# First quarter of w_ada by row blocks on an encoder layer kernel, and ScalarE's statistics of x moved ahead

## The chip, the cores and the metric

The kernel runs on one core of one Trainium2 chip. The metric is the device time of one execution in microseconds (us); less is better. Each time in the text is of one core; nothing is shared with other cores.

## The reference, cut to what matters

One encoder layer with 512 tokens of width 1024, batch 1, all f32. What the change touches is the beginning:

```python
mod = jnp.einsum('bd,de->be', jax.nn.silu(c), w_ada[l]) + b_ada[l]      # c: (1, 1024), w_ada: (1024, 6144)
sh_a, sc_a, g_a, sh_f, sc_f, g_f = jnp.split(mod[:, None, :], 6, axis=-1)
h = _layer_norm(x) * (1.0 + sc_a) + sh_a                                # needs the first third of mod
proj = h @ w_in[l]                                                      # 512 x 1024 by 1024 x 3072
```

Behind it come eight heads of neighbourhood attention, four heads of differential attention, an output projection with a layer norm, and PEER: for each token and each of eight heads 16 experts are chosen, and their rows of two tables of 16384 x 1024 are gathered, multiplied and added up. The output is one (1, 512, 1024) array.

## The kernel before, in words

The five engines have a program each, written out by hand, and wait for one another by semaphores. TensorE goes through a list of groups (`FIRST_GROUPS`, lines 118 to 138): two small transposes (columns of c and b_ada, and the neighbourhood bias), four `na_table` groups of eight products of a 32 x 128 by a 32 x 60 block (L721), the eight transposed blocks of the normalised x (`h_act` and `h_dve`, L744), then the stream of projections of w_in and "ada" groups, then attention. Each group has one of six banks of PSUM in turn, and it may start when the group that had the bank before has been evacuated by ScalarE or VectorE (`wait_for_bank`, L645). From the gather phase on, the expert rows come by indirect DMA issued by GpSimd (L623), VectorE makes the dot products (L1379) and TensorE the weighted sums (L837).

**Weights.** w_ada is 1024 x 6144, cut into twelve chunks of 512 columns (2 MB each), and w_in into six. They go through five slots of SBUF in the order of `STREAM` (L59 to 61): w_ada's chunks 0 to 3, then a chunk of w_in, two of w_ada, and so on. SP issues the loads (`load_chunk`, L467). A chunk is laid out as eight blocks of 128 rows side by side, so each partition gets eight runs of 512 f32 (2 KB). Chunks 0 to 3 are the first 2048 columns: sh_a and sc_a. Their slots are free for the next loads when the semaphore `mod_summed` is up (L461).

**The first 2048 columns of mod.** VectorE sums each chunk over its eight row blocks, each times its column of silu(c) (`sum_chunk`, L1202): one `tensor_scalar` (L1210) and seven `scalar_tensor_tensor` (L1212) of 128 x 512, each linked to the one before by a semaphore. The sums still have to be added up over the 128 partitions, and shift and scale are wanted as columns: that is `mod_columns` (L636), four products a chunk of a 128 x 128 block of the sum with a column of ones, each of which writes one column of `mod_ps` (L640). An f32 product stands as two instructions in the profile. It comes in TensorE's program behind the group ("h_dve", 6), and when chunk 3 is through, `mod_summed` rises. VectorE adds b_ada (L1230, L1231), `mod_ready` rises, and ScalarE and VectorE evacuate the transposed blocks of x with the scale and the shift in them (L968, L1252). The first projection (L754) takes them as they come, and needs the first chunk of w_in.

**Statistics of x.** ScalarE's own queue carries, before anything else, the loads of `na_place`, of the four 128-row tiles of x (L866), of `t5_place`, `t5_bias` and the sub-keys. Tiles 0 and 1 have their mean and variance from VectorE (L1068, L1221; the semaphore is `x_agg`). Tiles 2 and 3 have them from ScalarE: in front of the evacuation of `na_table` 2, ScalarE sums the tiles (L954), waits for the mean from GpSimd (L565), sums the squares of the differences (L958), and then normalises all four tiles (L962) as GpSimd delivers shift and inverse deviation (L566 to L575). TensorE's transposes of x wait for the four normalised tiles (L741).

**Order on VectorE:** statistics of tiles 0 and 1, sums of chunks 0 to 3 (a small copy behind chunk 1), the addition of b_ada, the evacuations. **Order on SP:** small loads, five chunks, the lambda rows, and, once `na_table` 3 is through, `mods` (b_ada's other rows), then the further chunks as slots come free.

## Time and profile before

| | us |
|---|---|
| median of 3 runs | 1751.28 |
| lowest and highest of them | 1751.17, 1754.83 |
| profiled execution, span from its first to its last instruction | 1756.3 |
| TensorE busy | 1479.7 (84%) |
| VectorE busy | 1140.1 (65%) |
| GpSimd busy | 985.6 (56%) |
| ScalarE busy | 432.3 (25%) |

The profile is of one execution of its own; no other time of that execution is given than its span, which is 5.0 us above the median of the three runs. PE is TensorE's matmuls, PEld its weight loads, DVE is VectorE, ACT ScalarE, POOL GpSimd and SP SyncE; SPq and ACTq are the DMA issues in those engines' programs. The whole of the first quarter of w_ada, summed and turned into columns, lies in the first 50 us of the span; the stream of projections lies between about 48 and 225 us, attention behind it, and the gathers fill the rest from about 385 us on.

### The profile page before, as it was taken

The page shows a single profiled execution, that of the slowest core. Times are in us where ns is not written, and L with a number is a line of the kernel's source. Part 1 is how long each engine was busy: PE and PEld are TensorE (multiplying, and loading weights), DVE is VectorE, ACT ScalarE, POOL GpSimd, SP SyncE. Part 2 cuts the span into 40 slices and gives each one's busy share as a digit, 9 for nine tenths or more (in the row PEclk, how much of TensorE's full clock was granted, in tenths as well). Part 3 has the DMA queues.
Part 4 walks back from the last instruction along what each step waited for, and adds up shares of the span by engine and source line. Part 5 has one row for each costly group of instructions (what it writes and reads, how often), then busy time and mean ns, then how long its engine had stood idle before and what let it go on. Part 6 is the DMA issues. An engine that isn't in the chain of part 4 may idle for free.

```text
span 1756.3 us, 14526 instructions
## 1 busy us (share of the span) xinstructions
PE 1479.7 (84%) x4096; PEld 684.0 (39%) x4096; DVE 1140.1 (65%) x2797; ACT 432.3 (25%) x1096; POOL 985.6 (56%) x1055
## 2 busy tenths in 40 slices
PE   5999989879899989977798799987899777777776
PEld 5444455654454345422343344432344222222222
DVE  6543055777867657776767666776666766677753
ACT  2111142441322222222222222322222222222221
POOL 1000000036767757777776677777777777777771
PEclk9899997989999999999999999999999999999999
DMA  9869221069999999999999999999999999999993
GB/s 308 326 224 218 96 72 21 7 242 374 390 388 409 406 366 391 409 409 409 409 409 408 408 409 409 410 410 409 410 409 409 409 409 409 410 409 409 410 409 152
DMA packets 190679, 606.02 MB, mean 345 GB/s; under 512 B 30704, under 2 KB 31112, under 8 KB 190440
## 3 DMA queue, kind: packets, MB, share of 16 engines
q0 software_dynamic: 147456, 536.94, 77.1%
q1 hardware_dynamic: 41799, 64.29, 11.3%
q10 hardware_dynamic: 1344, 3.87, 0.8%
q8 instruction: 34, 0.56, 0.1%
q14 instruction: 46, 0.37, 0.1%
HBM read 601.68 MB, written 3.34 MB: 344 GB/s over the span
## 4 chain that ended last, share of the span: by engine, by line
DMA 40%; PE 27%; POOL 14%; DVE 11%; issue 7%; ACT 1%; SPq 0%; DVEq 0%; POOLq 0%; ACTq 0%
DMA big<-in_expert_down,expert_idx 14%; DMA big<-in_expert_up,expert_idx 13%; PE pair L633 12%; POOL big L623 11%; PE pair L837 9%; DMA region_v<-in_expert_down,expert_idx 6%; DMA region_v<-in_expert_up,expert_idx 6%; POOL region_v L623 3%; PE pair L691 3%; DVE big L1379 3%; DVE big L1212 1%; DMA big<-in_w_ada 1%; PE pair L665 1%; PE pair L785 1%; DVE region_v L1379 1%
## 5 line engine op out<-in xcount | busy, mean ns | idle before, releaser
L837 PE MATMUL pair<-big 128*128 128x512 f32 x1460 | 710.1, 610 | 159.7 <-DMA big<-in_expert_up,expert_idx 147.0
L1379 DVE CUSTOM_DVE_ANT_0 big<-big,pair 128x1024 f32<-128x1024 f32 x363 | 442.6, 1220 | 250.1 <-DMA big<-in_expert_down,expert_idx 245.7
L837 PEld LDWEIGHTS pair<-big 128*128 128x128 f32 x1460 | 252.0, 190 | 547.3 <-issue 502.7
L623 POOL DMA_INDIRECT big<-in_expert_down,expert_idx x363 | 344.3, 948 | 150.1 <-issue 91.8
L623 POOL DMA_INDIRECT big<-in_expert_up,expert_idx x365 | 348.4, 955 | 127.1 <-issue 79.5
L837 PE MATMUL pair<-region_v,big 128*128 128x512 f32 x588 | 284.2, 606 | 61.6 <-DMA region_v<-in_expert_up,expert_idx 58.6
L1379 DVE CUSTOM_DVE_ANT_0 region_v<-region_v,pair 128x1024 f32<-128x1024 f32 x149 | 181.5, 1220 | 100.3 <-DMA region_v<-in_expert_down,expert_idx 97.7
L1026 ACT ACTIVATE big<-ident,big 128x128 f32<-128x128 f32 x512 | 167.1, 391 | 311.2 <-DVE big L1336 311.2
L633 PE MATMUL pair<-big 128*128 128x512 f32 (+1 forms) x480 | 194.2, 599 | 0.0
L837 PEld LDWEIGHTS pair<-region_v,big 128*128 128x128 f32 x588 | 101.8, 190 | 208.1 <-issue 187.9
L582 POOL TENSOR_SCALAR small<-small 128x4 f32<-128x4 f32 (+1 forms) x6 | 1.4, 236 | 318.6 <-DVE small L1308 282.1
L623 POOL DMA_INDIRECT region_v<-in_expert_down,expert_idx x149 | 141.3, 948 | 62.9 <-issue 38.3
L623 POOL DMA_INDIRECT region_v<-in_expert_up,expert_idx x147 | 139.4, 948 | 55.3 <-issue 30.2
L889 ACT ACTIVATE big<-big 128x4 f32<-128x4 f32 x128 | 26.1, 204 | 505.5 <-DVE big L1379 505.5
L665 PE MATMUL pair<-big 128*128 128x256 f32 (+1 forms) x640 | 141.2, 338 | 0.8 <-ACT big L925 0.8
L665 PEld LDWEIGHTS pair<-big 128*128 128x128 f32 x640 | 104.6, 191 | 86.7 <-issue 85.1
L633 PEld LDWEIGHTS pair<-big 128*128 128x128 f32 (+1 forms) x480 | 84.3, 196 | 93.3 <-issue 91.7
L925 ACT ACTIVATE big<-pair 128x512 f32<-128x512 f32 (+2 forms) x74 | 33.5, 457 | 214.0 <-PE pair L665 107.8
L691 PE MATMUL pair<-big 128*128 128x512 f32 x128 | 65.0, 620 | 0.7 <-issue 0.7
L1212 DVE SCALAR_TENSOR_TENSOR big<-big,small 128x512 f32<-128x512 f32 x84 | 63.2, 752 | 3.0
L1003 ACT ACTIVATE big<-pair 128x512 f32<-128x512 f32 (+3 forms) x70 | 37.6, 540 | 109.9 <-PE pair L633 99.7
L944 ACT ACTIVATE big<-big,small 128x256 f32<-128x256 f32 (+1 forms) x64 | 39.1, 610 | 78.3 <-DVE small L1284 78.3
(148 smaller groups left out, 1029.4 us busy)
## 6 DMA issues: line engine op xcount, KB each, us to landing
big<-in_w_ada SPq DMA_DIRECT2D x12, 2048.0 KB, 18.2
big<-in_w_in SPq DMA_DIRECT2D x6, 2048.0 KB, 17.0
big<-in_w_query SPq DMA_DIRECT2D x5, 2048.0 KB, 18.9
big<-in_expert_up,expert_idx POOLq DMA_INDIRECT x365, 15.5
big<-in_expert_down,expert_idx POOLq DMA_INDIRECT x363, 15.3
big<-in_w_out SPq DMA_DIRECT2D x2, 2048.0 KB, 10.3
big<-na_scr SPq DMA_DIRECT2D x24, 128.0 KB, 5.0
region_v<-in_expert_down,expert_idx POOLq DMA_INDIRECT x149, 13.0
```

The source lines that it names most:

```text
L623: nc.gpsimd.indirect_dma_start(places[place], None, (expert_down if kind == "down" else expert_up)[0], bass.IndirectOffsetOnAxis(expert_id ...
L633: last = nc.tensor.matmul(ps, a, b, start=(i == 0), stop=(i == len(pairs) - 1))
L665: return nc.tensor.matmul(ps[:, 0:n * P], w_slot[query_slot(c, first)][:, k, b * P:(b + 1) * P], src, start=(k == 0), stop=(k == KB - 1))
L691: return nc.tensor.matmul(ps[:, :], src, w_slot[OUT_SLOT[s]][:, k, :], start=(k == 0), stop=(k == KB - 1))
L837: last = nc.tensor.matmul(pair[t % 2][:, s * HALF:(s + 1) * HALF], diag[:, j, :], places[place][:, s * HALF:(s + 1) * HALF], start=(h == 0 ...
L889: nc.scalar.activation(acts[:, head % 2, lo:lo + QUARTER], at_head(dots, head)[:, lo:lo + QUARTER], ACT.Gelu).then_inc(gelu_done, 1)
L925: nc.scalar.activation(dst, ps, ACT.Copy).then_inc(act_evac, 1)
L944: nc.scalar.activation(exps, raw, ACT.Exp, bias=row_min[:, slot:slot + 1], scale=-1.0, accum_out=row_sum[:, slot:slot + 1]).then_inc(exp_d ...
L1003: nc.scalar.activation(dst, ps, ACT.Copy, scale=scale).then_inc(act_evac, 1)
L1026: nc.scalar.activation(diag[:, j, :], ident[:, :], ACT.Copy, scale=weights[:, head % 2, j:j + 1]).then_inc(diag_done, 1)
L1212: last = v.scalar_tensor_tensor(out=acc, in0=w[:, k, :], scalar=c_exp[:, k:k + 1], in1=acc, op0=ALU.mult, op1=ALU.add)
L1379: v.tensor_tensor_reduce(out=places[place], in0=places[place], in1=u_cur[:, :], scale=1.0, scalar=0.0, op0=ALU.mult, op1=ALU.add, accum_ou ...
```

## The change

The first four chunks of w_ada, 1024 x 2048, are loaded as eight row blocks of 128 x 2048 (1 MB, each partition one run of 8 KB), each with its own semaphore `ada_in`. VectorE takes block 0 (one `tensor_scalar` of 128 x 2048), then the statistics of the x tiles 0 and 1, then blocks 1 to 6 (one `scalar_tensor_tensor` of 128 x 2048 each). Block 7 (`ADA_DIRECT`) isn't summed: TensorE multiplies its sixteen 128 x 128 pieces straight with silu(c)'s last column, and then the sixteen pieces of VectorE's sum with the column of ones; VectorE adds the two sets of columns and b_ada in three operations. ScalarE's sums of x are moved ahead of the evacuation of `na_table` 0, its squares ahead of that of `na_table` 1, and its normalisation ahead of that of `na_table` 3. The counts of the slots' semaphores and the names around them are adapted, among them the waits of the later w_ada sums (`i - ADA_FIRST + 2`).

```diff
--- before.py
+++ after.py
@@ -64,7 +64,16 @@
 HEAD_ORDER = [0, 1, 8, 2, 3, 9, 4, 5, 10, 6, 7, 11]
 ATT = [(t, h) for t in range(TILES) for h in HEAD_ORDER]
 LAST_NA = max(a for a, (_, h) in enumerate(ATT) if h < NA_HEADS)
-STREAM_LOADS = [len(range(i, CHUNKS, WSLOTS)) for i in range(WSLOTS)]
+ADA_DIRECT = KB - 1
+
+
+def loads_to(n):
+
+    return n // WSLOTS + (1 if n % WSLOTS >= ADA_FIRST else 0)
+
+
+LAST_CHUNK = [max(range(i, CHUNKS, WSLOTS)) for i in range(WSLOTS)]
+STREAM_LOADS = [loads_to(n) for n in LAST_CHUNK]
 NA_SLOT = 0
 T5_SLOT = 3
 OUT_SLOT = [2, 4]
@@ -303,7 +312,7 @@
 
         h_t = region_h[:, :].rearrange("p (k s) -> p k s", k=KB)
         mixed = region_h[:, :].rearrange("p (t d) -> p t d", t=TILES)
-        first_sum = region_h[:, 0:ADA_FIRST * HALF].rearrange("p (i n) -> p i n", i=ADA_FIRST)
+        first_sum = region_h[:, 0:ADA_FIRST * HALF]
         ln2_rows = mods[:, 1:3, :]
         qk_t = region_qw[:, 0:16 * HALF].rearrange("p (b s) -> p b s", s=HALF)
         na_stage = region_qw[:, 0:2 * NA_ROW].rearrange("p (g n) -> p g n", g=2)
@@ -319,6 +328,7 @@
         gate_arg = sb("gate_arg", [P, PEER_HEADS * TILES * TOPK])
         w_flat = [big[:, region_q + i * KB * HALF:region_q + (i + 1) * KB * HALF] for i in range(WSLOTS)]
         w_slot = [w.rearrange("p (k n) -> p k n", k=KB) for w in w_flat]
+        ada_rows = big[:, region_q:region_q + ADA_FIRST * KB * HALF].rearrange("p (k n) -> p k n", k=KB)
         t5_bias_sb = w_flat[T5_SLOT][:, 0:DIFF_HEADS * T5_SPAN].rearrange("p (h j) -> p h j", h=DIFF_HEADS)
 
         v_beside = w_flat[T5_SLOT][:, 3072:4096].rearrange("p (i d) -> p i d", i=2)
@@ -379,7 +389,7 @@
 
             return spare_bank if GROUPS[g] == ("h_dve", (6,)) else bank[bank_at(g)]
 
-        mod_ps = pair[3][:, 0:2 * KB]
+        mod_ps = pair[3][:, 0:4 * KB]
         spare_bank = pair[3][:, HALF:D]
 
 
...
@@ -460,7 +472,7 @@
                 if n < ADA_FIRST:
                     sp.wait_ge(mod_summed, 1)
                 elif kind == "ada":
-                    sp.wait_ge(ada_summed, i + 1)
+                    sp.wait_ge(ada_summed, i - ADA_FIRST + 2)
                 else:
                     sp.wait_ge(pe_group, INDEX[("proj", (n, i, 3))] + 1)
 
@@ -472,7 +484,9 @@
                 sp.dma_start(w_slot[n % WSLOTS], src.rearrange("(k p) n -> p k n", p=P))\
                   .then_inc(w_in_slot[n % WSLOTS], 16)
 
-            for n in range(WSLOTS):
+            for k in range(KB):
+                sp.dma_start(ada_rows[:, k, :], w_ada[0, k * P:(k + 1) * P, 0:ADA_FIRST * HALF]).then_inc(ada_in[k], 16)
+            for n in range(ADA_FIRST, WSLOTS):
                 load_chunk(n)
             for i, v in enumerate((lambda_q1, lambda_k1, lambda_q2, lambda_k2)):
                 sp.dma_start(lam_in[:, i, :], v[0].partition_broadcast(P)).then_inc(rows_in, 16)
...
@@ -633,11 +646,16 @@
                     last = nc.tensor.matmul(ps, a, b, start=(i == 0), stop=(i == len(pairs) - 1))
                 return last
 
-            def mod_columns(n):
-
-                pe.wait_ge(ada_summed, n + 1)
-                for b in range(4):
-                    last = nc.tensor.matmul(mod_ps[:, 4 * n + b:4 * n + b + 1], first_sum[:, n, b * P:(b + 1) * P],
+            def mod_columns():
+
+                pe.wait_ge(c_ready, 1)
+                pe.wait_ge(ada_in[ADA_DIRECT], 16)
+                for b in range(2 * KB):
+                    nc.tensor.matmul(mod_ps[:, b:b + 1], ada_rows[:, ADA_DIRECT, b * P:(b + 1) * P],
+                                            c_exp[:, ADA_DIRECT:KB], start=True, stop=True)
+                pe.wait_ge(ada_summed, 1)
+                for b in range(2 * KB):
+                    last = nc.tensor.matmul(mod_ps[:, 2 * KB + b:2 * KB + b + 1], first_sum[:, b * P:(b + 1) * P],
                                             ones[:, 0:1], start=True, stop=True)
                 return last
 
...
@@ -817,9 +835,7 @@
                     last = key_products(ps, *args)
                 last.then_inc(pe_group, 1)
                 if kind == "h_dve" and args[0] == 6:
-                    for n in range(ADA_FIRST):
-                        last = mod_columns(n)
-                    last.then_inc(mod_summed, 1)
+                    mod_columns().then_inc(mod_summed, 1)
 
             for g in range(len(FIRST_GROUPS) - BANKS, len(FIRST_GROUPS)):
                 if bank_at(g) < 4:
@@ -948,15 +964,17 @@
                 if g == FIRST_PROJ:
                     act.wait_ge(lam_sum, 2)
                     nc.scalar.activation(lam, lam, ACT.Exp).then_inc(lam_exp, 1)
-                if kind == "na_table" and args[0] == 2:
+                if kind == "na_table" and args[0] == 0:
                     for t in range(2, TILES):
                         act.wait_ge(x_in[t], 16)
                         nc.scalar.activation(x_norm[:, t, :], x_sb[:, t, :], ACT.Copy,
                                              accum_out=x_sums[:, 0, t:t + 1]).then_inc(row_summed, 1)
+                elif kind == "na_table" and args[0] == 1:
                     act.wait_ge(mean_ready, 1)
                     for t in range(2, TILES):
                         nc.scalar.activation(x_norm[:, t, :], x_sb[:, t, :], ACT.Square, bias=mean4[:, t:t + 1],
                                              accum_out=x_sums[:, 1, t:t + 1]).then_inc(sq_summed, 1)
+                elif kind == "na_table" and args[0] == 3:
                     for t in range(TILES):
                         act.wait_ge(shift_ready, 1 + t // 2)
                         nc.scalar.activation(x_norm[:, t, :], x_sb[:, t, :], ACT.Identity, bias=shift4[:, t:t + 1],
@@ -1197,15 +1215,29 @@
             dve.wait_ge(c_exp_done, 1)
             link(v.tensor_scalar_add(c_exp, c_exp, 1.0))
             link(v.reciprocal(c_exp, c_exp))
-            link(v.tensor_tensor(c_exp, c_exp, c_col, ALU.mult))
+            v.tensor_tensor(c_exp, c_exp, c_col, ALU.mult).then_inc(c_ready, 1)
+            dve.wait_ge(c_ready, 1)
+
+            def sum_rows(k):
+
+                dve.wait_ge(ada_in[k], 16)
+                if k == 0:
+                    link(v.tensor_scalar(first_sum, ada_rows[:, k, :], c_exp[:, 0:1], None, ALU.mult))
+                else:
+                    last = v.scalar_tensor_tensor(out=first_sum, in0=ada_rows[:, k, :], scalar=c_exp[:, k:k + 1],
+                                                  in1=first_sum, op0=ALU.mult, op1=ALU.add)
+                    if k < ADA_DIRECT - 1:
+                        link(last)
+                    else:
+                        last.then_inc(ada_summed, 1)
 
             def sum_chunk(n):
 
                 at = STREAM.index(("ada", n))
-                dve.wait_ge(w_in_slot[at % WSLOTS], 16 * (at // WSLOTS + 1))
+                dve.wait_ge(w_in_slot[at % WSLOTS], 16 * loads_to(at))
                 if n >= ADA_FIRST + 2:
                     dve.wait_ge(dve_evac, EVAC[INDEX[("ada", (STREAM.index(("ada", n - 2)), n - 2, 0))]][1])
-                acc = first_sum[:, n, :] if n < ADA_FIRST else ada_sum[:, n % 2, :]
+                acc = ada_sum[:, n % 2, :]
                 w = w_slot[at % WSLOTS]
                 link(v.tensor_scalar(acc, w[:, 0, :], c_exp[:, 0:1], None, ALU.mult))
                 for k in range(1, KB):
@@ -1215,21 +1247,23 @@
                         link(last)
                 last.then_inc(ada_summed, 1)
 
+            sum_rows(0)
             for t in range(2):
                 dve.wait_ge(x_in[t], 16)
                 statistics(x_sb[:, t, :])
                 v.bn_aggr(x_mean_var[t], stats[:, :, :]).then_inc(x_agg, 1)
                 dve.wait_ge(x_agg, t + 1)
-            for n in range(ADA_FIRST):
-                sum_chunk(n)
-                if n == 1:
+            for k in range(1, ADA_DIRECT):
+                sum_rows(k)
+                if k == 1:
                     dve.wait_ge(t5_in, 32)
                     v.tensor_copy(t5_rep[:, :].rearrange("p (h r) -> p h r", h=DIFF_HEADS),
                                   t5_lhs.unsqueeze(2).to_broadcast([T5_BUCKETS, DIFF_HEADS, T5_COPIES])).then_inc(t5_ready, 1)
             dve.wait_ge(mod_summed, 1)
-            v.tensor_tensor(mod_cols[:, 0:KB], mod_ps[:, 0:KB], cols[:, KB:2 * KB], ALU.add)
-            v.scalar_tensor_tensor(out=mod_cols[:, KB:2 * KB], in0=mod_ps[:, KB:2 * KB], scalar=1.0,
-                                   in1=cols[:, 2 * KB:3 * KB], op0=ALU.add, op1=ALU.add).then_inc(mod_ready, 1)
+            link(v.tensor_tensor(mod_cols[:, :], mod_ps[:, 0:2 * KB], cols[:, KB:3 * KB], ALU.add))
+            v.tensor_tensor(mod_cols[:, 0:KB], mod_cols[:, 0:KB], mod_ps[:, 2 * KB:3 * KB], ALU.add)
+            v.scalar_tensor_tensor(out=mod_cols[:, KB:2 * KB], in0=mod_cols[:, KB:2 * KB], scalar=1.0,
+                                   in1=mod_ps[:, 3 * KB:4 * KB], op0=ALU.add, op1=ALU.add).then_inc(mod_ready, 1)
             dve.wait_ge(mod_ready, 1)
             dve.wait_ge(consts, 2)
             for g, (kind, args) in enumerate(FIRST_GROUPS):
```

## Rows read from the trace of the kernel before

**Rows 1.** The chain that ended last, whole span: start us, us, what.

```profile
57.83 22.45 PE pair L633 x52
80.66 144.22 PE pair L633 x336
```

**Rows 2.** The page, the span in 40 equal slices.

```profile
GB/s 308 326 224 218 96 72 21 7 242 374 390 388 409 406 366 391 409 409 409 409 409 408 408 409 409 410 410 409 410 409 409 409 409 409 410 409 409 410 409 152
```

**Rows 3.** The chain that ended last, from 0 to 60 us.

```profile
2.04 18.33 DMA big<-in_w_ada
...
44.33 1.88 PE pair L640 x8
...
48.52 9.31 PE pair L754 x16
```

**Rows 4.** Stretches: length, busy us by engine, PEclk, DMA share, GB/s.

```profile
10.00:14.00 4.00, 4.00 (x21) 4.00 (x20) 2.42 (x6) 0.57 (x1) 0.00 (x0) 1.00 1.04 269
...
22.00:36.00 14.00, 7.30 (x49) 6.98 (x48) 13.43 (x20) 5.47 (x6) 1.99 (x3) 1.00 1.05 387
```

**Rows 5.** The timeline of 0 to 80 us: start us, us, engine, line, what.

```profile
9.03 13.87 PE L721 MATMUL pair<-big,mods 32*128 32x60 f32 x64 [0.53 <-DVE big L1196]
...
16.11 0.57 ACT L1003 ACTIVATE big<-pair 128x480 f32<-128x480 f32 x1 [2.84 <-PE pair L721]
16.57 1.05 ACT L954 ACTIVATE region_v<-x_sb 128x1024 f32<-128x1024 f32 x1
...
21.72 6.06 SPq L472 DMA_DIRECT2D big<-in_w_in  x1
21.82 4.73 ACT L962 ACTIVATE region_v<-x_sb,shift,small 128x1024 f32<-128x1024 f32 x4 [0.24 <-POOL shift L571]
...
26.70 4.57 PE L744 MATMUL pair<-ident,region_v 128*128 128x128 f32 x28 [3.80 <-ACT region_v L962]
...
48.31 9.52 PE L754 MATMUL pair<-big 128*128 128x512 f32 x16
...
57.67 20.76 PE L633 MATMUL pair<-big 128*128 128x512 f32 x48
```

**Rows 6.** DMA issues of 21.7 to 22 us: KB each, us to landing.

```profile
big<-in_w_in SPq DMA_DIRECT2D x1, 2048.0 KB, 21.3
```

**Rows 7.** Groups on VectorE, shapes apart: count, busy us, mean ns, idle before.

```profile
L1212 DVE SCALAR_TENSOR_TENSOR big<-big,small 128x512 f32<-128x512 f32 x84 | 63.2, 752 | 3.0
...
L1090 DVE SCALAR_TENSOR_TENSOR x_sb<-x_sb,small,big 128x1024 f32<-128x1024 f32 x4 | 5.1, 1282 | 0.0
```

**Rows 8.** DMA queues, 5 to 15 us: packets, MB, share (q10 is ScalarE's, q1 SP's).

```profile
q10 hardware_dynamic: 485, 1.73, 67.7%
q1 hardware_dynamic: 528, 0.85, 36.9%
```

**Rows 9.** The tile x_sb, 0 to 30 us: issue and landing.

```profile
L866 ACTq DMA_DIRECT2D x_sb<-in_x x4: 611/653/810, 1.2 to 3.2; - x4
...
DMA to landing us min/median/max: 5.7/8.9/13.0
```

**Rows 10.** Groups of weight loads: 12 to 15, 32.4 to 33.6, 38 to 41 us.

```profile
L721 PEld LDWEIGHTS pair<-big,mods 32*128 32x128 f32 x16 | 3.5, 328 | 0.0
...
L640 PEld LDWEIGHTS pair<-big 128*128 128x128 f32 x8 | 1.0, 191 | 0.5 <-DVE big L1212 0.5
...
L640 PEld LDWEIGHTS pair<-big 128*128 128x128 f32 x8 | 1.8, 328 | 5.0 <-DVE big L1212 5.0
```

**Rows 11.** Stretches of 2 us, columns as in rows 4: the granted clock.

```profile
38.00:40.00 2.00, 1.58 (x8) 1.58 (x8) 1.93 (x4) 0.00 (x0) 0.00 (x0) 0.50 1.05 387
...
52.00:54.00 2.00, 2.00 (x4) 0.78 (x4) 0.00 (x0) 0.00 (x0) 0.00 (x0) 0.67 1.05 408
54.00:56.00 2.00, 2.00 (x6) 0.81 (x5) 0.00 (x0) 0.00 (x0) 0.00 (x0) 1.00 1.05 388
```

More of the change, by code:

```diff
@@ L406, in build @@
         w_in_slot = [sem(f"w_in_slot{i}") for i in range(WSLOTS)]
+        ada_in = [sem(f"ada_in{k}") for k in range(KB)]
         pe_group = sem("pe_group")
@@ L419, in build @@
         c_exp_done = sem("c_exp_done")
+        c_ready = sem("c_ready")
         shift_ready = sem("shift_ready")
@@ L497, in load_na_bias @@
                       .then_inc(na_bias_in[NA_LOAD[t]], 16)
-            last_chunk = [i + WSLOTS * (STREAM_LOADS[i] - 1) for i in range(WSLOTS)]
-            chunk_used(last_chunk[NA_SLOT])
+            chunk_used(LAST_CHUNK[NA_SLOT])
             sp.wait_ge(na_written, 16)
@@ L503, in _ @@
             load_na_bias(1, 1)
-            chunk_used(last_chunk[T5_SLOT])
+            chunk_used(LAST_CHUNK[T5_SLOT])
             sp.wait_ge(t5_written, 16)
@@ L509, in _ @@
                                      [[D - 1, COLS], [T5_COPIES * D, DIFF_HEADS], [1, T5_SPAN]])).then_inc(t5_bias_in, 16)
-            chunk_used(last_chunk[QUERY_SLOT[0]])
+            chunk_used(LAST_CHUNK[QUERY_SLOT[0]])
             sp.dma_start(w_slot[QUERY_SLOT[0]], w_query[0, :, 0:HALF].rearrange("(k p) n -> p k n", p=P))\
@@ L513, in _ @@
             for i, slot in reversed(list(enumerate(OUT_SLOT))):
-                chunk_used(last_chunk[slot])
+                chunk_used(LAST_CHUNK[slot])
                 sp.dma_start(w_slot[slot], w_out[0, :, i * HALF:(i + 1) * HALF]
@@ L735, in _ @@
                     _, i, _ = args
-                    pe.wait_ge(ada_summed, i + 1)
+                    pe.wait_ge(ada_summed, i - ADA_FIRST + 2)
                     last = product(ps[:, :], [(ones, ada_sum[:, i % 2, :])])
@@ L747, in _ @@
                     if b == 0:
-                        pe.wait_ge(w_in_slot[n % WSLOTS], 16 * (n // WSLOTS + 1))
+                        pe.wait_ge(w_in_slot[n % WSLOTS], 16 * loads_to(n))
                     w = w_slot[n % WSLOTS]
```

## The prediction

> **What bounds the kernel now.** I read the whole chain of waits first. From 57.8 us on it is TensorE's projections without a break (22.45 us and 144.22 us in one piece) [rows 1], then attention, then the gathers, whose data rate stands at about 409 GB/s in most of the later slices [rows 2]. So the projections start a long queue in which nothing waits for an absolute time: whatever moves their start moves the end by about as much. That makes the first 50 us the place to look. There the chain has the first chunk of w_ada in flight from 2.04 for 18.33 us, then VectorE's sums up to 44.3, then 1.88 us of TensorE's columns from 44.33 on, then the first projection at 48.52 [rows 3]. VectorE is thus the bound between 20.4 and 44.3: 13.43 of the 14 us from 22 to 36 are busy, while the DMA engines run at 387 GB/s [rows 4]. The DMA is close behind: the first chunk of w_in is issued at 21.72 [rows 5] and takes 21.3 us to land [rows 6], so it is in at 43.0. Had the sums cost nothing, the projections could not have started before that (48.5 now): some 5 us is the most to be won if the loads stay as fast as they are.
>
> **What goes.** Four sums of eight instructions, and with them the wait for the whole first chunk. The new sum of one block is 2048 wide. The 512-wide instruction has 752 ns, the 1024-wide one 1282 ns [rows 7]; the slope of 530 ns per 512 gives 2.34 us for 2048, estimated. Blocks land more than 2.3 us apart (1 MB at 387 GB/s [rows 4] is 2.7 us), so VectorE keeps up and its last sum ends about 2.4 us after block 6, when block 7 lands. The bound VectorE is gone; I cost its work at nothing, its cover being the DMA. If the cover fails by 0.1 us a block, six blocks cost 0.6 us. The first block's product is a single-source one and shorter; it goes ahead of the statistics of x on VectorE, which is why x_agg comes late: below.
>
> **When block 7 lands.** The old fourth chunk lands 5.4 us (2 MB at 387 GB/s) before w_in: 37.6. The new packets are 8 KB instead of 2 KB. The nearest row for large packets is the gathers' 409 GB/s [rows 2]: 8.4 MB take 20.5 instead of 21.7 us, so 36.4. In the first 18 us both queues run together and only at 269 GB/s [rows 4]; between 5 and 15 us they moved 528 and 485 packets [rows 8], that is one each in turn, a pair in some 0.38 us per engine. If what a pair loses against 387 GB/s (0.14 us) does not grow with the packet, the mixed stretch speeds up too and block 7 is in at 34.8. Ends: 34.8 and 37.6; I take 35.5. The first w_in chunk follows 5.4 us behind, about 41, and stops nothing.
>
> **When TensorE is free for the columns.** Its order is: tables, transposes of x for k = 0 to 6, then the columns. One packet in turn means that the x loads, 4 KB a packet, now share with 8 KB packets in place of 2 KB. The last tile of x is issued at 3.2 and lands 13.0 us later [rows 9], near 16; by my estimate 8.5 us of that lay in the mixed stretch, in pairs of 0.38 us. With pairs of 0.60 us (the same 0.14 us lost) it lands near 20.5, with everything doubled near 24. In the old order ScalarE went from the first sum of x at 16.57 to the last normalisation at 26.55 and TensorE's transposes started at 26.70 [rows 5]: 10.1 us. In the new order one sum (1.05 us) is done before the last tile lands, three evacuations of tables (0.57 us each [rows 5], part of them beside GpSimd's steps) come in between, so 10.4 us: transposes from 30.9, and 4.57 us long [rows 5], to 35.5. The statistics are moved ahead in ScalarE's queue, but they gain nothing, since x and, through x_agg, block 0 are what they wait for. Behind the waiting ScalarE stand the four evacuations of tables; TensorE needs their banks only for transposes that wait for the same x. No further cost. So columns start at 35.5, by both roads.
>
> **What the columns cost.** Before, the tail had four of them (8 instructions); now all 32 products wait for block 7 or for the sum, and as each f32 product is two instructions, 64 stand in a row. In the trace the eight at 44.33 take 1.88 us [rows 3]. Of the earlier sets, one at the slow pace had weight loads of 328 ns, 1.8 us for eight, and one at the fast pace 191 ns, 1.0 us for eight; the tables' loads, with TensorE at work all the time from 9.0 to 22.9 [rows 5], had 328 as well [rows 10]. Start to start that is 0.210 us against 0.116, worked out as the busy time less one load over seven. The granted clock in the stretch of the 328 ns at 38 to 40 is 0.50 [rows 11], the lower level of 1.2 GHz; the tables, though dense, ran at loads of the same length. [...] The fast set came right behind the transposes. Later, with only short sets between pauses, the clock was low, and it rose again near 54, after 5.7 us of full projections from 48.3 [rows 5, 11]. In the new order TensorE stands from 22.9 to 30.9, twice as long as the 3.8 us before the old transposes. I take the lower level: 63 × 0.210 + 0.36 (the last product) = 13.6 us. The ends are 7.5 us (0.116) and 13.6.
>
> The Trainium skill (TensorE: Matmul & The Clock Gate, section LDWEIGHTS) gives a weight load as its columns over 1.2 GHz at either clock, about 107 ns for 128 columns. By that the 64 would cost an estimated 6.8 us, half of my term; the rows of 328 and 191 ns speak against it, and no row of this kernel shows a load of 107 ns.
>
> **Small terms.** VectorE's part behind the columns has three operations with one link in place of two: +0.2 us. The mods load is freed by the last table (at 22.9) but stood behind SP's long issues; now it goes out at 23 and stands behind w_in, where nothing waits for it. Chunks 5 to 8 are issued when the columns are done, as before, and the next projection chunk is needed 27 us later: 0. Eight issues in place of four on SP: 0, as the queues hold.
>
> **Sum.** Columns done: 35.5 + 13.6 = 49.1, plus 0.2 = 49.3, against 44.33 + 1.88 = 46.2 now: +3.1 us. The first projections start at the same low clock as now: 0. The profiled execution has a span of 1756.3 us, 5.0 above the median of 1751.28; the difference of +3.1 is made within that execution and I carry it over to the median: **1754.4 us**. What a measurement of this kernel can tell from no change is 0.2%, 3.5 us.
>
> **Rivals.**
> - The likeliest (0.33, with a third of it beyond +3.5): as summed, +1 to +5.
> - **The clock has risen by the end of the transposes** (0.22). For: it did in the trace, and now the columns follow at once. Against: it was up at 32.4 and low by 38 in the trace, though columns had run until 33.4. Some 40 of the 64 at 0.116 and 24 at 0.210 make 9.7 us, so 35.5 + 9.7 + 0.2 − 46.2 = −0.8 us: 1750.5.
> - **The dense columns count as work for the clock** (0.24): 128-row loads back to back, which the tables (32 rows) were not. Then 7.5 us at best, and the first projection of 9.52 us runs in the 6.9 us that a later one takes (20.76 for three) [rows 5]: 35.5 + 7.5 + 0.2 − 46.2 − 2.6 = −5.6 us: 1745.7. The skill's figure for a weight load would lead to much the same time.
> - **x late** (0.21): the place is the last tile's landing on the second queue, and it decides from 20.5 us on, microsecond for microsecond. If pairs take twice as long, it lands at 24, the columns start at 39 and +6.6 us comes out: 1757.9; with 22.5, 1756.4. For: the one-for-one turns of [rows 8]. Against: no row shows a pair of 8 KB and 4 KB. The skill (DMA: Bandwidth & Descriptors, Arbitration) has each engine take turns between the queues by packet, not by bytes; by that rule, the trace agrees, x loses share when w_ada's packets grow.
>
> **How the numbers follow.** Faster by over 0.2%: all of the third case and a little of the second, 0.25. Slower: the fourth less a part, and the upper third of the first with some of the high landings, 0.33. Same: 0.42. The range goes from 1745.5 (the dense columns at the fast clock) to 1757.5 (x late), leaving out the outer parts of both; the likeliest case alone spans 1752 to 1757.
>
> **What would show it.** In the changed profile: the sums of L1212's successor at about 2.34 us and ending within 3 us of block 7; the last x tile landing at 19 to 22; transposes from about 31; 64 column instructions with loads near 328 ns in 13 us; columns done near 49. I am wrong if the loads show 191 ns over the whole row, if the columns start before 33, or if the first projection starts before 46.

## The result, and the profile after

The changed kernel takes 1762.59 us (median of 5 runs, 1760.47 to 1763.56), the kernel before in the same set 1751.91 (5 runs, 1751.17 to 1754.83). The ratio is 1.0046 with an interval from 1.0034 to 1.0059: slower by 8.1 us by the ratio, by 10.7 by the medians, and above the predicted range either way. The profiled execution's span is 1761.6 us, and its own time 1763.56. The busy times hardly moved (TensorE 1484.8 us, VectorE 1132.9, GpSimd 993.3, ScalarE 432.5); the loss is a later start.

The chain of waits of the changed kernel, from the last tile of x to the columns (start, length, what; all in us). It answers to [rows 3]:

```profile
3.19 19.16 DMA x_sb<-in_x
...
22.37 1.16 ACT region_v L970 x2
...
24.82 2.41 POOL small L582
...
27.30 2.83 POOL small L583
...
30.20 1.77 POOL shift L584
...
32.05 2.31 POOL small L586
...
34.44 2.82 POOL small L587
...
37.32 0.20 POOL shift L588
...
37.55 2.38 ACT region_v L980 x2
...
40.06 5.00 PE pair L762 x28
45.07 4.67 PE pair L654 x32
49.74 6.84 PE pair L658 x32
```

Before, this chain went through w_ada's first chunk and VectorE's sums. Now neither is in it. It waits for the last tile of x, then goes through GpSimd, then through TensorE's transposes (L762) and its 64 column instructions (L654 are the direct ones, L658 those of the sum). What strikes the eye is GpSimd: five instructions on 128 x 1 or 128 x 2 elements that take 1.8 to 2.8 us each. The timeline of the same kernel shows what ran beside them:

```profile
24.22 0.22 POOL L582 TENSOR_SCALAR small<-small 128x1 f32<-128x1 f32 x1
...
24.81 11.88 DVE L1227 SCALAR_TENSOR_TENSOR big<-big,small 128x2048 f32<-128x2048 f32 x5
24.82 2.40 POOL L582 TENSOR_SCALAR small<-small 128x1 f32<-128x1 f32 x1
...
32.00 2.37 ACT L980 ACTIVATE region_v<-x_sb,shift,small 128x1024 f32<-128x1024 f32 x2 [4.74 <-POOL shift L584]
...
37.55 2.37 ACT L980 ACTIVATE region_v<-x_sb,shift,small 128x1024 f32<-128x1024 f32 x2 [3.17 <-POOL shift L588]
...
58.89 7.96 PE L772 MATMUL pair<-big 128*128 128x512 f32 x16
```

The same instruction (L582, 128 x 1) takes 0.22 us at 24.22 and 2.40 us at 24.82. Between the two, at 24.81, VectorE has begun its row of five 2048-wide sums, 2.38 us each, and from there on GpSimd's simple steps end where a sum ends: 27.22 (sums end at 24.81 + 2.38 = 27.19), 31.97 (31.94), 34.35 (34.31). The two power steps (L583, L587) end 0.56 us behind the end of a sum, at 30.12 and 37.25. When the row is over, at 36.7, the step L588 takes 0.20 us. ScalarE, which normalises x with GpSimd's results, is idle for 4.74 and 3.17 us.

The columns by stretch (start and end, length, then busy us and number of instructions of PE, PEld, DVE, ACT, POOL, then the granted clock, the DMA share, GB/s):

```profile
44.00:46.00 2.00, 2.00 (x21) 2.00 (x19) 0.00 (x0) 0.00 (x0) 0.00 (x0) 1.00 1.00 416
...
48.00:50.00 2.00, 2.00 (x11) 2.00 (x11) 0.00 (x0) 0.00 (x0) 0.00 (x0) 0.50 0.36 147
...
60.00:62.00 2.00, 2.00 (x5) 0.77 (x5) 1.37 (x8) 0.20 (x1) 0.00 (x0) 0.81 1.05 410
```

The granted clock is at 2.4 GHz when the columns begin, falls within them (0.77 from 46 to 48), and is at 1.2 GHz until after the first projection has begun at 58.89 (0.50 from 58 to 60, 0.81 from 60 to 62).

The later milestones show where the delay stays and where it shrinks: columns done at 56.56 (before 46.2, +10.4), first projection at 58.89 (48.31, +10.6), next at 66.68 (57.67, +9.0), because the first one ran in 7.96 us in place of 9.52 [rows 5]. The stream of projections carries +9.0 unchanged to the first attention scores (234.65 against 225.64). At the first gathers it is +7.5 (356.3 against 348.8), and the two spans are 5.3 apart. The last two figures compare single executions, and the one before was 5.0 us above its median, so of the shrinking after the scores I can't say what is real.

### The profile page after: what moved, and what is told of

It reads as the page before. It is cut to its first block, busy times and chain, and to the rows that moved or that the text cites. A ratio compares the mean times of both kernels' runs of the same rounds, so it can differ in the third digit from the quotient of the medians.

```text
span 1761.6 us, 14577 instructions
## 1 busy us (share of the span) xinstructions
PE 1484.8 (84%) x4128; PEld 690.6 (39%) x4128; DVE 1132.9 (64%) x2773; ACT 432.5 (25%) x1096; POOL 993.3 (56%) x1055
## 4 chain that ended last, share of the span: by engine, by line
DMA 37%; PE 29%; POOL 17%; issue 8%; DVE 8%; ACT 1%; ACTq 0%; DVEq 0%; POOLq 0%
POOL big L636 12%; PE pair L646 12%; DMA big<-in_expert_up,expert_idx 11%; DMA big<-in_expert_down,expert_idx 10%; PE pair L853 10%; DMA region_v<-in_expert_up,expert_idx 9%; DMA region_v<-in_expert_down,expert_idx 6%; POOL region_v L636 4%; PE pair L709 3%; DVE big L1413 2%; PE pair L683 1%; DMA x_sb<-in_x 1%; PE pair L803 1%; DVE region_v L1413 1%; DVE big L1318 1%
## 5 line engine op out<-in xcount | busy, mean ns | idle before, releaser
L1318 DVE CUSTOM_DVE_ANT_1 big<-pair,big 128x256 f32<-128x256 f32 x32 | 13.3, 419 | 60.4 <-PE pair L792 60.2
```

The costliest lines, as they stand in the source:

```text
L1318: v.tensor_tensor_reduce(out=dst, in0=scored, in1=bias, scale=1.0, scalar=3.0e38, op0=ALU.add, op1=ALU.min, accum_out=row_min[:, slot:slot ...
```

## The experiments

There are twelve experiments, four at a time, each four on one chip and beside the kernel before. That kernel took 1753.98 us on the first chip (median of 26 runs; one of them, at 5075.40 us, is not in the ratios), but 1876.03 (29 runs) and 1864.48 (23 runs) on the two others, where the gathers ran slower: between 700 and 1400 us e5 has 371 GB/s, with a granted clock of 0.96 and 0.92, where e1 on the first chip has 409 GB/s and 1.00. Ratios are therefore compared within a set only; the first 60 us look alike on all three chips. The only trace of the kernel before is from its first timing. "Columns done" is the end of the last column product.

| kernel | transposes start | columns done | first projection | ratio to before |
|---|---|---|---|---|
| before | 26.7 | 46.2 | 48.31 | |
| after | 40.06 | 56.56 | 58.89 | 1.0046 [1.0034, 1.0059] |
| e1_sum512 | 32.49 | 49.02 | 51.35 | 1.0006 [0.9995, 1.0017] |
| e2_hold | 32.23 | 48.75 | 51.07 | 1.0018 [1.0007, 1.0028] |
| e3_no_direct | 41.84 | 51.54 | 53.66 | 1.0018 [1.0005, 1.0031] |
| e4_x_first | 39.44 | 55.98 | 58.29 | 1.0056 [1.0038, 1.0074] |
| e5_x_first_512 (2nd chip) | 32.73 | 46.11 | 48.43 | 1.0036 [1.0023, 1.0049] |
| e6_old_act (2nd) | 40.54 | 57.04 | 59.36 | 1.0055 [1.0031, 1.0079] |
| e7_before_new_act (2nd) | 25.73 | 46.15 | 48.26 | 1.0006 [0.9989, 1.0024] |
| e8_best (2nd) | 24.19 | 44.03 | 46.14 | 0.9976 [0.9957, 0.9995] |
| e8_again (3rd) | 24.09 | 44.18 | 46.30 | 0.9996 [0.9983, 1.0008] |
| e9_best_warm (3rd) | 24.66 | 41.68 | 43.79 | 0.9995 [0.9982, 1.0008] |
| after_again (3rd) | 40.62 | 57.15 | 59.48 | 1.0064 [1.0039, 1.0090] |
| e10_sum1024 (3rd, one execution) | 36.85 | 50.23 | 52.55 | |

My theory after the result was that GpSimd's steps are held up while VectorE runs a wide sum. The rivals were the late tile of x, and the row of columns itself.

**e1_sum512: the same sums in narrow pieces.** The bytes, the arithmetic and the order stay.

```diff
-                    last = v.scalar_tensor_tensor(out=first_sum, in0=ada_rows[:, k, :], scalar=c_exp[:, k:k + 1],
-                                                  in1=first_sum, op0=ALU.mult, op1=ALU.add)
+                    for lo in range(0, 2048, 512):
+                        part = slice(lo, lo + 512)
+                        last = v.scalar_tensor_tensor(out=first_sum[:, part], in0=ada_rows[:, k, part], ...)
```

> The changed kernel with VectorE's sums of blocks 1 to 6 cut into four instructions of 512 columns each (all else as changed). Theory (a GpSimd step cannot end while a wide two-input sum runs on VectorE; in the changed kernel six of its eight steps took 1.8 to 2.8 us instead of 0.2 to 1.2): the steps fall to at most 1.2 us, the transposes of x start at 32 to 34 us instead of 40.1 although the sums themselves get longer (3.15 us a block), the columns are done at 47 to 50 instead of 56.6, time 1754 to 1757. Rival (the lateness is all the x loads' landing at 22.4 and the order on ScalarE): transposes stay near 40, time stays near 1762.

(The trace of the changed kernel has ten GpSimd steps in this stretch, of which five took 1.8 to 2.8 us, and not six of eight.)

The timeline of this kernel, the same stretch:

```profile
22.35 1.06 ACT L970 ACTIVATE region_v<-x_sb 128x1024 f32<-128x1024 f32 x1 [4.22 <-DMA x_sb<-in_x]
...
24.39 13.82 DVE L1229 SCALAR_TENSOR_TENSOR big<-big,small 128x512 f32<-128x512 f32 x20
...
25.28 0.58 POOL L582 TENSOR_SCALAR small<-small 128x1 f32<-128x1 f32 x1
25.95 1.10 POOL L583 TENSOR_TENSOR small<-small 128x2 f32<-128x2 f32 x1
...
27.40 0.55 POOL L586 TENSOR_SCALAR small<-x_sums 128x2 f32<-128x2 f32 x1
...
32.49 5.82 PE L762 MATMUL pair<-ident,region_v 128*128 128x128 f32 x28 [10.68 <-ACT region_v L980]
38.15 4.05 PE L654 MATMUL pair<-small,big 128*128 128x1 f32 x32
42.06 6.96 PE L658 MATMUL pair<-big 128*128 128x1 f32 x32
```

The last tile of x comes at the same moment (22.35 and 22.37), and VectorE is even busier (13.82 us for the work of 11.88). But GpSimd's longest step is 1.10 us, the transposes start 7.6 us earlier, the columns are done 7.5 us earlier, and the time is that of the kernel before within its interval. One edit that changes only the width of VectorE's instructions gives back most of the loss.

**e2_hold: the wide sums stay, but not beside GpSimd.** VectorE waits with block 2 until GpSimd is through.

```diff
             for k in range(1, ADA_DIRECT):
+                if k == 2:
+                    dve.wait_ge(shift_ready, 2)
                 sum_rows(k)
```

> The changed kernel; VectorE waits for GpSimd's last step (shift_ready 2) before it sums block 2, so that no sum runs beside GpSimd's steps. Theory: all GpSimd steps at 0.2 to 0.7 us, the last done near 28, transposes from about 32 to 37, sums of blocks 2 to 6 from 28 to 40, columns done at 46 to 48, time 1752 to 1755, although VectorE was given a wait. Rival (GpSimd's steps are slow for another reason, or don't matter): the wait only costs, the time is 1762 or more.

Its timeline:

```profile
25.11 0.21 POOL L582 TENSOR_SCALAR small<-small 128x1 f32<-128x1 f32 x1
25.41 0.73 POOL L583 TENSOR_TENSOR small<-small 128x2 f32<-128x2 f32 x1
...
27.79 0.20 POOL L588 TENSOR_TENSOR shift<-mean,small 128x2 f32<-128x2 f32 x1
28.02 11.90 DVE L1227 SCALAR_TENSOR_TENSOR big<-big,small 128x2048 f32<-128x2048 f32 x5 [3.12 <-POOL shift L588]
```

GpSimd's steps are back at 0.2 and 0.7 us although the sums are as wide as in the changed kernel, and the transposes start at 32.23. The price is a VectorE that ends at 39.92 in place of 36.7; nobody waits for it, since TensorE is with the direct columns until 41.8. So it is the overlap in time that costs, and not the width by itself. The columns are done at 48.75 and the time is 3.2 us above the kernel before, both a little later than expected.

**e3_no_direct: VectorE sums block 7 too, and TensorE has 32 column instructions.** (VectorE's addition behind the columns goes back to two operations; the diff here leaves that out.)

```diff
-ADA_DIRECT = KB - 1
+ADA_DIRECT = KB
...
-                for b in range(2 * KB):
-                    nc.tensor.matmul(mod_ps[:, b:b + 1], ada_rows[:, ADA_DIRECT, b * P:(b + 1) * P],
-                                            c_exp[:, ADA_DIRECT:KB], start=True, stop=True)
```

> The changed kernel with block 7 summed by VectorE too, so that TensorE has 32 column instructions instead of 64. Theory (the columns stand in series behind the transposes, 4.8 us for the first 32): the sum of block 7 ends at 39.1, before the transposes do (45.1), so the columns are done 4.8 us earlier, near 51.5, time 1757 to 1759. Rival (the direct columns cost nothing, since TensorE would wait for VectorE in their place): 1762.

Its timeline:

```profile
24.96 14.27 DVE L1223 SCALAR_TENSOR_TENSOR big<-big,small 128x2048 f32<-128x2048 f32 x6
...
37.47 1.81 POOL L588 TENSOR_TENSOR shift<-mean,small 128x2 f32<-128x2 f32 x1
...
41.84 6.13 PE L758 MATMUL pair<-ident,region_v 128*128 128x128 f32 x28 [19.37 <-ACT region_v L976]
47.80 3.74 PE L654 MATMUL pair<-big 128*128 128x1 f32 x32
```

The seventh sum also holds GpSimd's last step (1.81 us in place of 0.20), so the transposes are 1.8 us later than in the changed kernel, and still the columns are done 5.0 us earlier. The 32 instructions that are gone took 4.7 us; the 32 that are left take 3.74 us in place of 6.96, mostly at the high clock; the later and slower transposes (6.13 us against 5.00) take 2.9 of it back. VectorE's last sum ends at 39.2, 8.6 us before TensorE is free. The direct product of block 7 was meant to save VectorE's last step; that step was hidden, and its replacement lay on the path.

**e4_x_first: the loads of x on SP's queue, ahead of w_ada.**

```diff
-            for t in range(TILES):
-                nc.scalar.dma_start(x_sb[:, t, :], by_column(x)[t]).then_inc(x_in[t], 16)
...
+            for t in range(TILES):
+                sp.dma_start(x_sb[:, t, :], by_column(x)[t]).then_inc(x_in[t], 16)
```

> The changed kernel with the four x loads issued by SP ahead of the w_ada blocks, in one queue, instead of by ScalarE beside them. Theory (8 KB packets take the turns of the 4 KB packets of x): the last x tile lands by 15 instead of 22.4, block 7 near 36 as before, transposes of x from 29 to 36 (GpSimd's steps still blocked in part by the wide sums), columns done at 47 to 52, time 1753 to 1758. Rival (x is slow by itself, its rows far apart in memory): x still lands after 18 us and pushes w_ada and w_in back by as much; time at 1760 or above.

The last tile of x is used at 14.58, 7.8 us earlier than in the changed kernel, and the transposes start only 0.6 us earlier. Its timeline shows why:

```profile
14.58 1.06 ACT L970 ACTIVATE region_v<-x_sb 128x1024 f32<-128x1024 f32 x1 [1.13 <-DMA x_sb<-in_x]
...
16.94 1.29 DVE L1225 TENSOR_SCALAR big<-big,small 128x2048 f32<-128x2048 f32 x1 [10.41 <-DMA big<-in_w_ada]
...
21.43 0.22 POOL L583 TENSOR_SCALAR mean<-small 128x1 f32<-128x1 f32 x1 [5.27 <-DVE small L1254]
21.74 2.10 POOL L584 TENSOR_SCALAR small<-small 128x1 f32<-128x1 f32 x1
...
26.40 2.30 POOL L584 TENSOR_SCALAR small<-small 128x1 f32<-128x1 f32 x1
```

Tiles 0 and 1 have their statistics from VectorE, which first takes block 0 of w_ada; that now lands later (the product starts at 16.94 in place of 13.38). GpSimd goes on at 21.43 after 5.27 us of waiting for them, and then its steps fall beside wide sums again. The late tile alone was worth nothing: two other things stood right behind it. The expected landing came true (by 15), the rest did not: the columns were done at 55.98 in place of 47 to 52, and the time is the rival's, 1764.00, though not for the rival's reason.

**e5_x_first_512: e4 and e1 together** (both diffs above).

> The changed kernel with both edits at once: x loads ahead of w_ada in SP's queue, and VectorE's sums cut to 512 columns. x first alone left the time where it was, for GpSimd's steps took 14 us beside the wide sums. Theory (wide sums hold GpSimd up, and only behind that does the landing of x count): GpSimd's steps end near 27.5, transposes start near 30 and end near 35, columns wait for block 7 (36 to 37) and are done at 46 to 49, time 1752 to 1756, some 8 us under x first alone. Rival (x is not on the path at all): the same as the narrow sums alone.

Columns done at 46.11, against 49.02 with the narrow sums alone, and the start is back to that of the kernel before. But the early x did not bring this. The transposes start no earlier (32.73 against 32.49, where about 30 was expected), as the rival has it. As in e4, tiles 0 and 1 wait behind block 0, and one step of GpSimd takes far longer than one sum:

```profile
25.16 2.25 POOL L586 TENSOR_TENSOR shift<-mean,small 128x2 f32<-128x2 f32 x1
```

The sums beside it begin every 0.69 us from 24.63 on. It ends at 27.41, with the third sum that began after it, so a step can lose more than one sum; why this one did is not found. The 2.9 us lie in TensorE's own work. From the start of the transposes to the last column it needs 13.38 us here and 16.53 in e1; the granted clock falls later: 1.00 from 40 to 42 us, where e1 has 0.80. e10 below, without the early x, needs 13.38 as well, and the changed kernel, e2, e4 and e6 need 16.5, so no edit here explains which of the two it is.

The time does not follow: the ratio of 1.0036 is 6.8 us, on a chip where one run of before differs from another by up to 15 us. The first attention scores start at 225.47 (before 225.64) and the first gather at 346.45 (348.77), so what costs this lies behind the start of the gathers. It is not found.

**e6_old_act and e7_before_new_act: ScalarE's order by itself,** once put back in the changed kernel, once put into the kernel before.

```diff
-                if kind == "na_table" and args[0] == 0:
+                if kind == "na_table" and args[0] == 2:
```

(That is e6 at its first line; the squares and the normalisation then follow in the same branch, and e7 has the reverse.)

> The changed kernel with ScalarE's order as before (all its work on x in front of the evacuation of na_table 2), the row blocks kept. Theory (the order on ScalarE is worth nothing where x lands at 22.4 and GpSimd is held up): columns done at 56 to 57, time within 1 us of the changed kernel's 1762. Rival (the order itself costs, as the table evacuations stand behind the wait for x): several us faster than 1762.

> The kernel before with only the new order on ScalarE. Theory: its statistics come earlier, and GpSimd's steps, from 16 to 19, run before VectorE's first sum at 20.5, so they take 0.2 to 0.7 us each; the transposes start at 23 to 24 instead of 26.7, but the columns wait for VectorE's sums to 44.3 either way: no change of the time, 1751 to 1754. Rival: some us to be had by the order alone.

With the old order in the changed kernel the transposes start at 40.54 and the columns are done at 57.04, as good as equal to the changed kernel's 40.06 and 56.56. With the new order in the kernel before they start at 25.73 (1 us earlier; 23 to 24 was expected), the columns are done at 46.15, and the ratio is 1.0006. The order is worth nothing that can be measured in either place.

**e8_best and e8_again: what the first experiments point to.** x first on SP, its statistics ahead of block 0 on VectorE, all eight blocks summed by VectorE in pieces of 512, and TensorE's columns following the last block's pieces. The diff shows parts of this.

```diff
+            for t in range(TILES):
+                sp.dma_start(x_sb[:, t, :], by_column(x)[t]).then_inc(x_in[t], 16)
...
+                    if b % 4 == 0:
+                        pe.wait_ge(part_summed, b // 4 + 1)
...
-            sum_rows(0)
             for t in range(2):
...
+            sum_rows(0)
```

> A version meant to beat both: x loads first in SP's queue; VectorE takes the statistics of tiles 0 and 1 ahead of block 0, sums all eight blocks in 512-column pieces, and TensorE's columns follow the last block's pieces one by one (32 instructions, none for block 7 directly). Theory: GpSimd's steps end by 20, transposes by 28, block 7 lands at 36 to 37, the last piece is summed at 39 to 40, columns done at 41 to 43, first projection at 43 to 45 (w_in lands near 41 to 42), time 1746 to 1750. Rival (w_in's landing, or something else in the first 45 us, bounds the start): at 1750 or above.

> The same version as in the call before (x first, statistics before block 0, all blocks summed in 512-column pieces, columns behind the last block's pieces), again, since the chip of that call ran everything some 7% longer in the gathers. Theory: columns done at 44 instead of 46.2, first projection 2.1 us earlier than in the kernel before, so some 2 us faster (0.1%): 1749 to 1752 where the kernel before has 1752 to 1754. Rival: what the start gains is lost behind it: no difference.

Its timeline, and then its stretches:

```profile
22.32 16.59 DVE L1227 SCALAR_TENSOR_TENSOR big<-big,small 128x512 f32<-128x512 f32 x24
24.19 5.27 PE L762 MATMUL pair<-ident,region_v 128*128 128x128 f32 x28 [4.53 <-ACT region_v L978]
37.07 6.96 PE L658 MATMUL pair<-big 128*128 128x1 f32 x32 [7.61 <-DVE big L1227]
```

```profile
40.00:42.00 2.00, 2.00 (x11) 2.00 (x11) 0.00 (x0) 0.00 (x0) 0.00 (x0) 0.50 0.44 171
```

The transposes are out of the way by 29.5, but now TensorE stands for 7.6 us, the clock falls to 1.2 GHz, and 32 columns cost 6.96 us. They are done at 44.03, 2.2 us ahead of the kernel before, where 41 to 43 was expected. The ratio is 0.9976 [0.9957, 0.9995] on the one chip and 0.9996 [0.9983, 1.0008] on the other: a gain clear of the noise once, and none that could be told the second time.

**e9_best_warm: e8 with work for TensorE in the pause.** Eleven products of a 128 x 128 by a 128 x 384 block are added whose result nobody reads.

```diff
+                for _ in range(11):
+                    nc.tensor.matmul(pair[3][:, P:HALF], ident[:, :], x_norm[:, 0, 0:HALF - P], start=True, stop=True)
```

> That version with eleven products of 128 x 384 on data that nobody reads, put between the transposes and the columns, where TensorE stood idle for 7.6 us; their results go to a free part of a PSUM bank. Theory (the row of small products neither raises nor holds the clock, and full products do): the columns' weight loads fall from 328 to 191 ns, the 32 instructions follow the last block's pieces and are done near 40 to 41, the first projection starts at 42 to 43 at the high clock, time 4 to 7 us under the kernel before. Rival (the clock falls again within the columns as it did in the changed kernel, or the idle products delay the columns): columns done at 43 or later, no more than 3 us gained.

Its timeline and its stretches:

```profile
17.24 0.22 POOL L584 TENSOR_SCALAR mean<-small 128x1 f32<-128x1 f32 x1
17.41 1.29 DVE L1225 TENSOR_SCALAR big<-big,small 128x2048 f32<-128x2048 f32 x1 [5.29 <-DMA big<-in_w_ada]
17.54 1.23 POOL L585 TENSOR_SCALAR small<-small 128x1 f32<-128x1 f32 x1
...
29.09 7.26 PE L656 MATMUL pair<-region_v,ident 128*128 128x384 f32 x22
...
37.73 3.95 PE L660 MATMUL pair<-big 128*128 128x1 f32 x32 [1.37 <-DVE big L1229]
```

```profile
38.00:40.00 2.00, 2.00 (x20) 2.00 (x20) 1.66 (x3) 0.00 (x0) 0.00 (x0) 1.00 0.81 264
40.00:42.00 2.00, 1.67 (x14) 1.58 (x13) 0.25 (x3) 0.00 (x0) 0.00 (x0) 0.77 0.49 190
```

The columns take 3.95 us in place of 6.96, and the first projection starts 4.5 us before that of the kernel before. The clock falls in the columns all the same, so that the projection takes 9.09 us. Columns done at 41.68 and a first projection at 43.79 lie a little behind what was expected. The time was to be 4 to 7 us under the kernel before, and isn't: the ratio is 0.9995, that is -0.9 us with an interval from -3.4 to +1.5. Beside the trace of before, this one is 5.0 us ahead at the first attention scores (220.68 against 225.64) and 7.2 us at the first gather (341.62 against 348.77). So by these two traces the lead is there when the gathers begin, and by the interval a part of it at least is gone at the end.

**after_again and e10_sum1024.** The changed kernel once more beside these, and the sums in pieces of 1024 (the diff of e1 with 1024 for 512, one execution).

> The changed kernel as it is, beside the others on the same chip. Theory: 9 to 11 us above the kernel before, as in its first timing (1762.59 against 1751.91), GpSimd's steps at 1.8 to 2.8 us beside the wide sums again. Rival (part of the gap was that chip): clearly less.

> The changed kernel with the sums of blocks 1 to 6 in two instructions of 1024 columns. Theory (a GpSimd step ends when the VectorE instruction that runs beside it ends): the single-input steps of GpSimd, 0.6 to 0.7 us beside sums of 512 columns and 2.3 to 2.4 us beside sums of 2048, stand at 1.1 to 1.3 us, transposes start at 34 to 36. Rival (they are slowed by VectorE's activity in general, not by the length of an instruction): the same as beside 2048 columns.

The changed kernel is slower by 1.0064 on this chip too. The 1024-wide pieces lie in between: transposes at 36.85, a little behind the 34 to 36 expected. One step of GpSimd against the width of the sums beside it (L586, a `tensor_scalar` of 128 x 2, and L587, the power):

| VectorE beside it | one sum | L586 | L587 |
|---|---|---|---|
| nothing (e2) | | 0.19 | 0.69 |
| 512 wide (e1) | 0.69 | 0.55 | 1.08 |
| 1024 wide (e10) | 1.25 | 1.23 | 1.61 |
| 2048 wide (after) | 2.38 | 2.30 | 2.81 |

The simple step takes nearly as long as the sum, at each width, and the power some 0.4 us more than the sum.

## Why the prediction was wrong, point by point

**What bounds the kernel before** and how a later start travels to the end: right for this change. The first projections start 10.6 us later, and the time rises by 8.1 (ratio) to 10.7 us (medians). In the first set of four the times follow the start roughly: first projection at +3.0, +2.8, +5.4 and +10.0 (e1 to e4) with +1, +3, +3 and +10 us by the ratios. As a rule it fails on the other chips: e5 starts 0.1 us later and costs 6.8 us, e9 starts 4.5 us earlier and gains at most 3.4. "Whatever moves their start moves the end by about as much" holds up to the gathers; through them the runs show it clearly only for the starts that lie 10 us later (the changed kernel and e4).

**VectorE's sums:** right in size, 2.38 us against the 2.34 estimated, and right in that VectorE is off the path. Costing its work at nothing looked only at when its sums end. It did not look at whom they hold up.

**When block 7 lands:** taken as 35.5. It was there by 36.85 at the latest, since e3's sum of it starts then without a pause. Nothing waited for it.

**x late:** the fourth case was right in kind. Against 20.5 taken, the last tile landed at 22.35 (3.19 + 19.16), inside my bounds; that is 1.85 us of the miss. Most of it is arithmetic of mine. 8.5 us of pairs of 0.38 us are 22.4 pairs; at 0.60 us each they move the landing from 16.2 to 21.1, not 20.5. With 387 GB/s kept throughout (0.13 us lost, pairs of 0.635) it is 21.9. The DMA queues from 5 to 15 us, against [rows 8]:

```profile
q1 hardware_dynamic: 366, 1.78, 63.2%
q10 hardware_dynamic: 303, 1.09, 39.9%
```

q1, with w_ada, moves 1.78 MB (before 0.85), q10, with x, 1.09 MB (before 1.73): x lost share as described. But e4 shows that this alone decided nothing.

**From the landing of x to the transposes ("so 10.4 us: transposes from 30.9", "No further cost"):** this is the step that failed. It measured 17.7 us (22.35 to 40.06), 7.3 more. I took the chain ScalarE, GpSimd, ScalarE from the kernel before with its durations, and there GpSimd's steps were short: five were over before VectorE's first sum began at 20.46, and the sums beside the others were 512 wide. The 2048-wide sums of the changed kernel held five steps up for 1.8 to 2.8 us each. Even so, the trace of before had the sign. Its groups of instructions on GpSimd between 14 and 30 us:

```profile
L574 POOL TENSOR_TENSOR small<-small 128x2 f32<-128x2 f32 x1 | 1.2, 1204 | 0.1
L570 POOL TENSOR_TENSOR small<-small 128x2 f32<-128x2 f32 x1 | 0.7, 727 | 0.1
L573 POOL TENSOR_SCALAR small<-x_sums 128x2 f32<-128x2 f32 x1 | 0.7, 700 | 0.1
...
L569 POOL TENSOR_SCALAR small<-small 128x1 f32<-128x1 f32 x2 | 0.4, 216 | 0.2
```

The same power step took 0.73 us once and 1.20 the other time, and a `tensor_scalar` 0.70 where its likes take 0.22. I did not ask why. With the sums narrow (e1) the stretch is 10.1 us, with the sums held (e2) 9.6: about my figure, once the overlap is gone or short.

**The columns:** taken as 13.6 us at the low clock, they took 11.65 (4.7 direct and 7.0 of the sum): the weight loads were down to 191 ns by the end of the transposes, and the clock fell in the row. That the 328 ns of the tables' loads stood for the lower level was a wrong reading: the granted clock from 10 to 14 us is 1.00 [rows 4]. The second case had this mechanism, at 9.7 us. It came true in part, and its forecast of a gain did not, since the columns began 9.4 us later (44.91 against 35.5). The third case, in which dense columns count as work for the clock, fell: the granted clock falls while they run back to back in the changed kernel and in e9, and in e8, where it was at 0.50 before them, it stays there for their 7 us.

The sum, put right: 30.9 + 1.85 (x) + 7.3 (GpSimd) = 40.06; the transposes up to the first column 4.85 in place of 4.6; the columns 11.65; together 56.56, against 49.1 predicted and 46.2 before.

**The signs of being wrong** that I had named (loads of 191 ns over the whole row, columns before 33, a first projection before 46) all looked for an earlier start. None of them appeared, and none could have shown this miss.

**What the change was worth without GpSimd's part:** e2, and nearly so e1, are that kernel. They start 2.8 and 3.0 us later than before, near the +3.1 of the sum, though out of other terms (x 1.85 later, the columns shorter). The direct product of block 7 costs 5.0 us in the changed kernel (e3).

**What is open:** the 6.8 us of e5, which its start does not explain; what becomes of the earlier starts of e8 and e9 in the gathers; and why TensorE's stretch from the transposes to the last column takes 13.4 us in two kernels and 16.5 in the others that have 64 column instructions.

## What to carry to other kernels

When an instruction on VectorE is made wider, look at what GpSimd runs beside it: here a chain of tiny GpSimd steps paid up to the length of a whole VectorE instruction at each link, so sum in narrow pieces there, or let the chain finish first. Moving work from an engine that isn't last to finish onto the one that is (block 7 onto TensorE) lies on the path in full. And when one of two queues got larger packets (8 KB in place of 2), the other's last load took 19.2 us to land in place of 13.0: check which of them starts the longer chain of work.

## What the runs showed of the hardware

A GpSimd instruction on one or two elements a partition that meets a VectorE instruction of the kinds below does not end before it. This holds for the two-input sums at three widths (0.55, 1.23, 2.30 us beside 0.69, 1.25, 2.38). It holds in e9 for the one-input product of block 0 as well: L585 takes 1.23 us beside L1225's 1.29, and 0.22 without it. Once, in e5, a step outlasted three further sums (2.25 us beside sums of 0.69). VectorE isn't slowed: five sums take 11.88 us beside GpSimd and 11.90 alone (e2).

The Trainium skill states this rule (SBUF — State Buffer, section Who interferes with whom): the two engines share a pair of ports, as an exclusive lock. A VectorE instruction with two inputs in SBUF contends for it with a GpSimd instruction that reads SBUF, and so does one in a fast two-port mode, where whoever issues first has the pair for the whole instruction and the other blocks fully. The traces agree for both kinds, with the figures above; the product of block 0 moves 2048 elements in 1.29 us where a sum takes 2.35, which fits such a fast mode. Had I held this rule against GpSimd's steps, the missing 7.3 us could have been priced ahead.

While TensorE ran products of one column, back to back, its granted clock fell: it was 1.00 when they began and 0.50 from 48 us on in the changed kernel. In e9 it was 1.00 through the products 384 wide and fell after the columns had begun. At the low clock 32 column instructions take 6.96 us, at the high one mostly 3.6 to 4. A granted clock of 1.00 alone does not make a load short: the tables' loads take 328 ns at it [rows 4, 10].
